# State space mixer rebuilt: parameters made in earlier stages, input scaled after its transfer through memory, three of its four quarters by GpSimd

## The reference, cut to what matters

```python
    return rmsnorm(x, final_g)
...
def s5_mixer(x, a_re, a_im, log_dt, b_re, b_im, c_re, c_im, d_skip, w_glu, w_out):
    u = x.astype(f32).reshape(bsz, seq, SSM_GROUPS, SSM_GROUP)      
    dt = jnp.exp(log_dt.astype(f32))[:, None]
    lam_re = jnp.minimum(a_re.astype(f32), -1e-4)
    mag = jnp.exp(lam_re * dt)
    lbar_re, lbar_im = mag * jnp.cos(lam_im * dt), mag * jnp.sin(lam_im * dt)
...
    y = y.reshape(bsz, seq, D_MODEL) + d_skip.astype(f32) * x.astype(f32)
    h = jax.nn.gelu(y)
    val, gate = jnp.split(h @ w_glu, 2, axis=-1)
    z = val * jax.nn.sigmoid(gate)
```

## Time and profile before

| | us |
|---|---|
| median of 3 runs (lowest, highest) | 4406.85 (4403.81, 4413.22) |
| the profiled execution | 4410.32 |
| its span on the core | 4408.5 |
| TensorE / VectorE / ScalarE / GpSimd busy | 4083.4 / 1918.9 / 1275.7 / 1491.3 |

### The profile page before, as it was taken

One profiled execution on the slowest core, in us unless ns is written; L12 is line 12 of the kernel. 1 busy time (PEld: TensorE's weight loads), 2 busy tenths in 40 slices (PEclk: granted clock), 3 DMA queues, 4 the chain that ended last, 5 costly groups with the idle time before them and its releaser, 6 DMA issues.

```text
span 4408.5 us, 51098 instructions
## 1 busy us (share of the span) xinstructions
PE 4083.4 (93%) x19931; PEld 3125.3 (71%) x19931; DVE 1918.9 (44%) x2148; ACT 1275.7 (29%) x1901; POOL 1491.3 (34%) x1022
## 2 busy tenths in 40 slices
PE   7998998899999989549999999998999999999998
PEld 5776774457777764448888888886666678888886
DVE  4254661326676761861263323314444455323321
ACT  3222330222222211321142232225444544223222
POOL 1430000011111118552344444443444444444443
PEclk8999999999999999779999999999999999999999
DMA  6111004311212131621223333331000022333333
GB/s 228 39 39 53 1 0 163 113 53 68 72 68 76 70 116 43 111 69 48 72 92 99 95 100 95 96 104 66 22 25 20 25 97 95 95 99 97 96 99 105
DMA packets 115674, 344.05 MB, mean 78 GB/s; under 512 B 17588, under 2 KB 35279, under 8 KB 113792
## 3 DMA queue, kind: packets, MB, share of 16 engines
q1 hardware_dynamic: 100368, 296.12, 21.6%
q0 software_dynamic: 7680, 31.54, 1.9%
q10 hardware_dynamic: 7472, 14.22, 0.9%
HBM read 315.37 MB, written 24.12 MB: 77 GB/s over the span
## 4 chain that ended last, share of the span: by engine, by line
PE 61%; issue 17%; DVE 9%; POOL 8%; ACT 2%; DMA 2%; POOLq 0%; ACTq 0%; SPq 0%; DVEq 0%
PE banks L274 21%; PE banks L2937 6%; POOL w_parts L259 6%; PE banks L1214 6%; PE banks L288 5%; PE banks L692 5%; PE banks L1572 4%; PE banks L978 3%; PE banks L3011 2%; DVE neg_max L1057 2%; PE banks L3040 1%; PE banks L3027 1%; PE banks L1553 1%; DMA w_ring<-in_weights 1%; PE banks L1602 1%
## 5 line engine op out<-in xcount | busy, mean ns | idle before, releaser
L259 POOL TENSOR_TENSOR w_parts<-w_ring,w_parts 128x1024 fp32r<-128x1024 f32 x344 | 835.3, 2429 | 1128.3 <-ACT w_parts L252 1128.3
L274 PE MATMUL banks<-x_high,w_parts 128*128 128x512 f32 x2944 | 911.9, 390 | 0.0
L252 ACT ACTIVATE w_parts<-w_ring 128x1024 fp32r<-128x1024 f32 x344 | 364.5, 1060 | 1292.1 <-PE banks L274 1284.7
L274 PEld LDWEIGHTS banks<-x_high,w_parts 128*128 128x128 f32 x2944 | 552.6, 188 | 116.5 <-issue 2.1
L274 PE MATMUL banks<-x_low,w_parts 128*128 128x512 f32 x1472 | 572.7, 389 | 0.0
L274 PE MATMUL banks<-hidden_high,w_parts 128*128 128x512 f32 x1600 | 482.0, 391 | 6.0 <-POOL w_parts L259 6.0
L3145 DVE TENSOR_TENSOR_SCAN arena<-arena,flags 128x128 f32<-128x128 f32 (+3 forms) x192 | 229.7, 1200 | 285.9 <-ACT arena L3086 284.4
L274 PEld LDWEIGHTS banks<-hidden_high,w_parts 128*128 128x128 f32 x1600 | 301.8, 189 | 70.9 <-POOL w_parts L259 6.8
L274 PEld LDWEIGHTS banks<-x_low,w_parts 128*128 128x128 f32 x1472 | 276.3, 188 | 59.3 <-issue 1.9
L1214 PE MATMUL banks<-parts_b,w_ring_low 128*128 128x512 f32 x896 | 303.7, 406 | 13.6 <-DVE resid_low L391 9.7
L2829 DVE TENSOR_TENSOR hidden_high<-banks,gate_temps 128x512 f32 (+1 forms) x88 | 60.9, 692 | 571.9 <-PE banks L274 571.8
(11 more groups left out here) (431 smaller groups left out, 6597.6 us busy)
## 6 DMA issues: line engine op xcount, KB each, us to landing
w_ring<-in_weights SPq DMA_DIRECT2D x488, 512.0 KB, 3.5
arena<-in_hy_dft SPq DMA_DIRECT2D x11, 1536.0 KB, 6.2
resid<-in_xT ACTq DMA_DIRECT2D x2, 2048.0 KB, 25.6
resid<-in_xT POOLq DMA_DIRECT2D x1, 4096.0 KB, 13.7
arena<-in_fn_seq POOLq DMA_DIRECT2D x1, 4096.0 KB, 17.2
resid_spill<-resid POOLq DMA_DIRECT2D x1, 4096.0 KB, 12.4
hidden<-resid_spill POOLq DMA_DIRECT2D x1, 4096.0 KB, 15.8
s_in<-hidden SPq DMA_DIRECT2D x4, 1024.0 KB, 9.8
```

Of the source, the lines that this page charges most:

```text
L252: nc.scalar.activation(WP[:, g % 2, 0, :], WR[:, (g % RING) * TILE:(g % RING + 1) * TILE], ACT.Identity).then_inc(w_hi, 1)
L259: nc.gpsimd.tensor_tensor(WP[:, g % 2, 1, :], WR[:, (g % RING) * TILE:(g % RING + 1) * TILE], WP[:, g % 2, 0, :].bitcast(F32), ALU.subtrac ...
L274: mm = nc.tensor.matmul(PS[:, bank + h // H, :], w[a][:, k % KB, :], srcs[b][:, k, at + h:at + h + H], start=(first and i + q == 0), stop= ...
```

## The change

- **Parameters early.** The computation of `S5Prep` moves from GpSimd at 1650 us to VectorE in `EvOut` (`denominator`, `angle`, `coefficients`, `powers_c(0)`, `steps`), before the norm `n_x1` (`phases(0)`) and in `Fourier` (the other quarters). GpSimd's queue keeps each result in DRAM (`keep`) and loads them back in `OdOut` and `S5`. The table `hy_dft` is loaded in `Fourier` after the last `keep`; before, at the start of `EvOut`.
- **Sums of squares.** VectorE adds the squares of `OdOut`'s tiles up; TensorE sums them once after the last tile, in token order and in the order by chunks (`RINV8`).
- **Scale late.** ScalarE writes the unscaled tiles (times `final_g`) into `R` right after each tile, and SP sends three quarters to memory during `OdOut`. They are read back into `XT`, and there multiplied by `RINV8`: quarter 0 by VectorE, quarters 1 to 3 by GpSimd (`normed`).
- **`inputs`** for all four quarters run in `OdOut`, into buffers of their own; the first `turned` stands before tile 7.
- **`ssm_d`** enters as 64 small products in `kernels`; the gelu is applied when the outputs are copied out; `skip` and the second gelu are gone.
- **Order of SP:** all reads of the inputs, then `toeplitz(0)`; for each quarter the outputs go out before `toeplitz(q+1)`.
- The residual for the layer norm goes to memory before the mixer (4 MB, GpSimd's queue) and comes home after it (SP's queue); VectorE scales it then.

```diff
@@ norm_stage, dve_parts (n_x1)
             def dve_parts(v_, link):
+                S5Prep.phases(v_, link, 0)
                 wait_done(v_, after)
...
@@ EvOut.dve, after tile n
+                if n == 0:
+                    S5Prep.denominator(v, link)
+                if n == 1:
+                    S5Prep.angle(v, link)
+                if n == 3:
+                    S5Prep.coefficients(v, link)
                 if n in (4, 6):
                     HyPrep.angles(v, link, n // 2 - 2)
+                if n == 4:
+                    S5Prep.powers_c(v, link, 0)
+                if n == 5:
+                    S5Prep.steps(v, link)
...
@@ HyPrep.pool, Fourier.pool
-            g.dma_start(ar(B_TAB, 8 * 512), ins["hy_dft"][:, 0:8 * 512]).then_inc(dft_in, 16)
+            S5Prep.params(g)
+            S5Prep.keep(g, "small")
+            S5Prep.keep(g, "cl", 0)
...
             for j in range(6):
                 Paired.weight_low(g, j)
+                if j in (2, 3, 4):
+                    S5Prep.keep(g, *(("cl", 1), ("e", 1), ("cl", 2))[j - 2])
+            S5Prep.keep(g, "e", 2)
+            S5Prep.keep(g, "cl", 3)
+            S5Prep.keep(g, "e", 3)
+            g.wait_ge(pre_kept, 48 + 64)
+            g.wait_ge(pre_kept_e, 64)
+            g.dma_start(ar(B_TAB, 8 * 512), ins["hy_dft"][:, 0:8 * 512]).then_inc(dft_in, 16)
...
@@ S5Prep
+        def keep(g, what, q=0):
+            k = ["small", ("cl", 0), ("e", 0), ("cl", 1), ("e", 1), ("cl", 2), ("e", 2), ("cl", 3), ("e", 3)]
+            g.wait_ge(pre_made, k.index((what, q) if what != "small" else what) + 1)
...
+            elif what == "cl":
+                g.dma_start(cl_dram[q], ar(22016, QP * 288)).then_inc(pre_kept, 16)
...
@@ Fourier.dve
+            S5Prep.powers_c(v, link, 1)
+            S5Prep.phases(v, link, 1)
+            S5Prep.powers_c(v, link, 2)
             for b in range(0, 8, 2):
                 v.wait_ge(f_ab, b + 1)
                 nc.vector.tensor_copy(FAB[:, b, :], PS[:, 4 + b % 4, :]).then_inc(f_abd, 1)
+            S5Prep.phases(v, link, 2)
+            S5Prep.powers_c(v, link, 3)
+            S5Prep.phases(v, link, 3)
...
@@ OdOut.pe
             for n in range(8):
                 matmul_tile(p, OdOut.st, n, n, M1)
-                if n:
-                    sums(n - 1)
-            sums(7)
+                if n == 6:
+                    S5.turned(p, 0)
+            p.wait_ge(s5_vbt, 4)
+            for i, sq in enumerate((ACC_SQ, SQ)):
...
+                for t in range(CK):
+                    mm = nc.tensor.matmul(PS[:, 4, 0:NC], PARTS_OF_ONES[:, 112 - 16 * t:240 - 16 * t], sq[:, t:T:CK],
+                                          start=(i + t == 0), stop=(i == 1 and t == CK - 1), skip_group_check=True)
...
@@ OdOut.act, after tile n
+                nc.scalar.activation(R[n // 2 % 2][:, n % 2, :].rearrange("p (s c) -> p s c", s=CK),
+                                     HT[:, n, :].rearrange("p (c s) -> p s c", s=CK), ACT.Identity,
+                                     scale=vec("final_g", n)).then_inc(s5_r, 1)
...
@@ OdOut.dve, after tile n
+                if 1 <= n <= 6:
+                    OdOut.waits(v, "sq_ready", n + 1)
+                    nc.vector.tensor_tensor(ACC_SQ, ACC_SQ, SQ[:, :], ALU.add).then_inc(n_sem["sq_free"], 1)
+                if n < 4:
+                    S5.inputs(v, link, n)
...
@@ S5.sp
+            for e in range(E0, E0 + 8 + RING):
+                load(e)
+                if e - E0 in (5, 7, 9):
+                    inputs_out((e - E0 - 5) // 2)
+            inputs_in(0)
+            inputs_out(3)
+            for q in range(1, 4):
+                inputs_in(q)
+            s.wait_ge(s5_zero, 4)
             toeplitz(0)
-            for q in range(4):
-                u_in_out(q)
+            s.wait_ge(spilled, 80)
             for q in range(4):
-                if q < 3:
-                    toeplitz(q + 1)
                 s.wait_ge(s5_ye, 4 * (q + 1))
...
+                if q < 3:
+                    toeplitz(q + 1)
+                s.wait_ge(y_out, 16 * CK * (q + 1))
...
+            s.dma_start(XT, spill).then_inc(x_home, 16)
 
@@ S5.pool
+            g.wait_ge(s5_vt, 4)
+            phases_in(1)
+            wait_done(g, OdOut.done)
+            g.dma_start(spill, HT).then_inc(spilled, 16)
+            OdOut.waits(g, "mean_in", 1)
+            magnitudes(0)
+            S5.normed(g, nc.gpsimd, 1)
+            S5.normed(g, nc.gpsimd, 2)
+            g.wait_ge(s5_vt, 8)
+            magnitudes(1)
+            S5.normed(g, nc.gpsimd, 3)
+            for q in (2, 3):
+                g.wait_ge(s5_st, q - 1)
+                phases_in(q)
+                magnitudes(q)
+                powers_in(q)
 
+        def normed(waits, engine, q):
+            waits.wait_ge(u_in, 16 * CK * (q + 1))
+            if q:
+                waits.wait_ge(s5_un, q)
+            u = XT_[:, 16 * q * NC:16 * (q + 1) * NC].rearrange("p (g c) -> p g c", g=16)
+            engine.tensor_tensor(u, u, RINV8.unsqueeze(1).broadcast_to([P, 16, NC]), ALU.mult).then_inc(s5_un, 1)
...
@@ S5.dve
+            link(nc.vector.reciprocal(RINV8, RINV8))
+            S5.normed(v, nc.vector, 0)
+            v.wait_ge(u_out, 64)
+            S5.chain(v, link, 0)
+            S5.chain(v, link, 1)
+            S5.chain(v, link, 2)
+            S5.chain(v, link, 3)
+            v.wait_ge(s5_st, 4)
+            for k in range(KB):
+                low(k)
+            link(nc.vector.reciprocal(RINV[:, :], RINV[:, :]))
+            v.wait_ge(x_home, 16)
+            for k in range(KB):
+                nc.vector.scalar_tensor_tensor(XT[:, k, :], XT[:, k, :], vec("final_g", k), RINV[:, :],
+                                               ALU.mult, ALU.mult).then_inc(n_sem["scaled"], 1)
...
@@ S5.act, in quarter 3 before its outputs
+                    a.wait_ge(s5_tp, 16 * CK * 4)
+                    for j in (-2, -1):
+                        round_ahead(a, PLAN["glu"], j)
+                    for k in range(4):
+                        high(k)
...
@@ S5.pe
+                    for par in range(2):
+                        b = 2 * par + j // 4
+                        mm = nc.tensor.matmul(PS[0:16, b, (j % 4) * P:(j % 4) * P + 16], IDENT[32:48, 32:48],
...
-                    return PS[:, 2 * par + j // 4, (j % 4) * NC:(j % 4 + 1) * NC]
+                    return PS[:, S5.bank(q) + 2 * par + j // 4, (j % 4) * NC:(j % 4 + 1) * NC]
```

More of the change, by code:

```diff
@@ L1279, in pool @@
             g.dma_start(spill, XT).then_inc(spilled, 16)
+            S5Prep.keep(g, "e", 0)
         def products(p, i):
@@ new lines, in _build @@
+    pw_dram = nc.dram_tensor("s5_pw", (P, 576), F32, kind="Internal").ap()
+    m8_dram = nc.dram_tensor("s5_m8", (P, 32), F32, kind="Internal").ap()
+    s5p_in, s5_ang, s5_sin = (sem("s5_" + x) for x in ("par", "ang", "sin"))
+    pre_made, pre_kept, pre_kept_e = (sem("s5_" + x) for x in ("made", "kept", "kept_e"))
+    s5_r, u_out, u_in, s5_zero, s5_un = (sem("s5_" + x) for x in ("r", "u_out", "u_in", "zero", "un"))
+    s5_cl, s5_e, s5_vb, s5_k, s5_km, s5_tp = (sem("s5_" + x) for x in ("cl", "e", "vb", "k", "km", "tp"))
@@ L1946, in _build @@
+    CLS = [ar(14848 + QP * 288 * i, QP * 288, **cl_shape) for i in range(2)]
+    ACC_SQ = ar(19456, T)
+    PARTS_OF_ONES = ar(20480, 240)
+    M8_, RINV8 = ar(20720, 32), ar(20752, NC)
+    RV, TV = ar(20976, 2048, **e_shape), ar(23024, 2048, **e_shape)
+    R = [ar(20976 + 2048 * i, 2048, "p (k t) -> p k t", k=2) for i in range(2)]
+    STT_ = ar(25072, 2 * QP * (NC + 1), "p (i j c) -> p i j c", i=2, j=QP)
+    TP = ar(27136, 2048, "p (g n) -> p g n", g=16)
     class OdOut(Stage):
@@ L2207, in _build @@
-    TCL = take(QP * 9 * 16)
-    S.insert(S.index(OdOut) + 1, S5Prep)
     class S5(Stage):
@@ L2350, in dve @@
-            low(7)
+            tt = nc.vector.tensor_tensor
+            def low(k):
+                v.wait_ge(s5_hi, k + 1)
+                if k == 3:
+                    v.wait_ge(s5_y, 16)
+                tt(PTA[:, 1, k, :].rearrange("p (c t) -> p c t", t=CK), HT[:, k, :].rearrange("p (t c) -> p c t", t=CK),
+                   PTA[:, 0, k, :].bitcast(F32).rearrange("p (c t) -> p c t", t=CK), ALU.subtract).then_inc(s5_part, 1)
+            OdOut.waits(v, "root", 1)
+            link(nc.vector.reciprocal(RINV8, RINV8))
@@ L2374, in act, with results @@
-            for k in range(KB):
-                OdOut.waits(a, "scaled", k + 1)
-                nc.scalar.activation(HT[:, k, :].rearrange("p (s c) -> p s c", s=CK),
-                                     XT[:, k, :].rearrange("p (c s) -> p s c", s=CK), ACT.Identity).then_inc(s5_r, 1)
+            def results(q):
+                for n, (b, g0) in enumerate(PARITY_BANKS):
+                    a.wait_ge(s5_y, 4 * q + n + 1)
+                    nc.scalar.activation(XT_[:, :].rearrange("p (g c) -> p g c", c=NC)[:, 16 * q + g0:16 * q + g0 + 7:2, :],
```

(12 more changed lines are left out.)

599 lines of the change are left out of this document (296 added, 303 removed).

## The result

| | before | after |
|---|---|---|
| median of 4 runs each (lowest, highest), us | 4408.67 (4403.81, 4413.22) | 4365.48 (4364.9, 4369.62) |
| span of the profiled execution, us | 4408.5 | 4363.0 |
| OdOut starts | 1650.5 | 1656.0 |
| T, end of the last tile | 1770.9 | 1767.9 |
| y0, y3 | 1835.3, 1953.5 | 1836.7, 1915.9 |

The ratio is 0.9904, with a 95% interval from 0.9887 to 0.9921: 1.0% faster. The forecast was 4354.0, so 11.5 us too low, and 7.3 us too low by the spans (4355.7 against 4363.0); the result lies inside the forecast's range, 4345 to 4366, by half a microsecond. By the marks: the front of the kernel loses 5.5, the tiles of `OdOut` give 8.5, T to y0 costs 4.5, the loop gives 39.1 and the tail 8.0, together -45.6; the spans differ by 45.5.

The account below looks back on a forecast made before the run. The mixer was where time must be earned: TensorE worked 91 of 170 us there. Gains 8.3 - 0.6 + 40.2 + 4.9 + 0 = 52.8 us, off the median 4406.85, gave 4354.0 us; own range 4345 to 4366.

Parts of the forecast that it names:

- Tiles: In OdOut, sums of squares leave the row of tiles and 16 transposes enter it: gain 8.3 us.
- The loop: From quarter 0's outputs to quarter 3's: GpSimd's waits go, SP's transfers bind; 78 us for 118.2, gain 40.2.
- T to y0: From OdOut's last tile to quarter 0's outputs: early input waits behind other reads; 65 us against 64.4, cost 0.6.
- issued to T + 51.5, landed at T + 54: In SP's queue after OdOut, toeplitz(0) stands behind all four input reads and lands 54 us after the last tile.
- The residual's part: After OdOut, the residual's 4 MB delay quarter 0's reading: back at T + 21, against T + 11 without contention.
- The scale on GpSimd: Beside the chains, GpSimd's scale takes 4.0 us against VectorE's 2.4 and is hidden; uncovered, 3 x 4 us.
- GpSimd and VectorE hinder each other: Rival in the chains: three GpSimd scales stretch VectorE's operations and come late, 13 us in all, 4367 us; chance 0.09.
- The tail: From quarter 3's outputs to the first Glu tile's end: 26.5 us against 31.4, gain 4.9.
- cold TensorE: In the tail, before the first Glu tile ends, a TensorE gone cold adds 2.5 us.
- The front: Early parameter steps and table load in EvOut, Fourier and before Hyena: 0 us net, from -3 to +6.
- pushes Hyena's first rows back 2 to 3 us: Just before Hyena, the 2 MB table hy_dft now loads and delays the stage's first rows by 2 to 3 us.
- 2 to 3 back: At EvOut's start, where the table no longer loads beside the weights, some 2 to 3 us are gained.

Follow-up runs that it names:

- e1: Changed kernel with quarters 1 to 3 scaled by VectorE, each after the previous quarter's chain, instead of by GpSimd: 4369.1 us, ratio to before 0.9906.
- e2: Changed kernel with toeplitz(0) issued ahead of the readings of quarters 1 to 3: 4359.0 us, ratio to before 0.9889.
- e5: Changed kernel with the table hy_dft loaded behind Hyena's first rows and W3 instead of ahead of them: 4363.7 us, ratio to before 0.9903.
- e8: Changed kernel with toeplitz(0) ahead of readings 1 to 3 and VectorE scaling inside the chains: 4351.3 us, ratio to before 0.9873.
- e9: Changed kernel with VectorE scaling inside chains, residual written in three pieces, toeplitz(0) between readings 2 and 3, hy_dft behind Hyena's first rows: 4345.6 us, ratio to before 0.9849.
- e3: Changed kernel with the residual's 4 MB sent after GpSimd's third scale instead of at T + 2: 4357.1 us, ratio to before 0.9884.

## Why the prediction was right, and where it wasn't

**Tiles.** -8.5 for -8.3: right, with tiles end to end and T 111.9 us after the start. No run undoes this part or the tail's; both rest on the rows alone.

**The loop.** 79.1 for 78, gain 39.1 for 40.2. Cause and size hold: putting GpSimd's work back costs 36.5. SP's writes and `toeplitz` run back to back and part 1 waits for them, 26.4 us apart on average for 26. In chains 2 and 3 no wait for GpSimd is left. That the number came so near is in part luck. From y to the start of part 1 a quarter took 18.5, 17.4 and 16.8 us for the 16.5 of the sum, 3.2 us more in all, and the products 26.4 for 28.5. And in the other profiles that leave the loop's work and order as they are (e1, e2, e5, e8, e9) it took 79.3 to 88.0.

**T to y0.** Forecast 65, measured 68.9. The step that failed is `toeplitz(0)` "issued to T + 51.5, landed at T + 54". Quarters 0 and 1 were back a little sooner than I put them (T + 19.9 for 21, T + 30.0 for 31), but quarters 2 and 3 later (T + 42.5 for 41, T + 54.1 for 51). SP was free for `toeplitz` at T + 46, while the last reading was still under way; its eight transfers then took 6.8 us to issue, which I had nearly left out, and landed 5.6 us after that, 4.5 after the last reading, where I had given 3. So of the 4.6 us that `toeplitz(0)` was late, 3.1 are the readings' and 1.5 its own. That the early input is spent behind the other reads is right: moving `toeplitz(0)` forward and taking GpSimd off the chain gave 10.7 us. The residual's part, 4 MB against the readings, is right in direction: 6 us by e3, for the 10 (T + 21 against T + 11) that the sum held. That quarter 0 came back near T + 21 is luck in part, since two errors nearly cancel: without the 4 MB it is back at T + 14 and not T + 11. Nor was the T + 23 of both transfers in full reached: the 4 MB took 19.6 us instead of 12.4, so both gave way.

**The scale on GpSimd.** It took 4.52 us, for 4.0. "Hidden" is right for this order (e1). The rival "GpSimd and VectorE hinder each other" named the right engines and the wrong mechanism. I stretched operations 2.9 times and got 2.6 us a scale, and 1.6 for GpSimd's lateness; in truth one operation is stopped until the scale is over, which alone costs 4.2. That my total, 3 x 4.2 = 13 us, meets the 12.6 measured on chain 0 is luck. It did become the bound, not in the changed kernel but in e2, where `toeplitz(0)` no longer was.

**The tail.** 23.5 for 26.5, gain 8.0 for 4.9. The steps up to the last reading back took 15.0 us for 15.1. After it the sum held 8.9 us for `high`, `low` and products, and 2.5 for a cold TensorE, together 11.4; measured, 8.5. TensorE had six of eight blocks done before, as it had before the change, and began the other two after one `high` and one `low` (3.9 us), with the second pair beside it; the sum counted both `high`. The cold TensorE was there: the last two blocks took 4.5 us (1934.81 to 1939.33) at a mean granted clock of 0.66, as they did before (4.54), and at the rate of the 22 products in the next 4.67 us, at full clock, their twelve would take 2.5. So that term was about right, by this estimate 2.0 for 2.5.

**The front.** Forecast 0, measured +5.5 between the two profiles, and it makes most of the miss. 2.3 of it is there before the change's first instruction: `EvOut` starts at 671.1 for 668.8. Over the eight profiles with this same front it starts at 668.0 to 671.7, so this is spread between executions. From `EvOut`'s start to `OdOut`'s took 981.7 us before and 978.5 to 985.3 in those eight, on average 983.2: 1.5 us more, with one profile of the kernel before to set against a spread of 7. The interval with the table's load, which varies far less (39.1 to 40.6 for 37.8 before), holds 2.1 more on average, and giving the rows the way takes 2 back: with the table behind, `EvOut` to `OdOut` took 981.3 on average of four. So the forecast's "pushes Hyena's first rows back 2 to 3 us" is right; what failed is the credit of "2 to 3 back" at the start of `EvOut`. Its first wait for weights fell from 8.60 us to 6.42, but a later one grew from 1.62 to 2.87, and no gain at its end can be told from the spread. The early steps themselves are covered: in `Fourier` two of the 18 operations of `powers_c` took 3.47 and 3.41 us beside `weight_low`, the others 1.36, and VectorE was free at 941.9, before the 944 asked for.

Together: +5.5 front, -0.2 tiles, +3.9 y0, +1.1 loop, -3.1 tail is 7.2 of the 7.3 us between forecast and span. The other 4.2 us of the miss on the median are the base: the forecast's median lay 1.7 us below its span, as the first runs of the kernel before had it, and the measured one lies 2.5 above.

## What to carry to other kernels

Before moving work to an engine off the path, look at what the path's engine will run beside it. GpSimd's scale was free while a transfer was late and cost 4.2 of its 4.5 us each time in the next version, once that transfer was in time. When a transfer stands in a queue behind others that aren't due, its place can cost more than its length: `toeplitz(0)`, 7 us long, came forward, the scale left GpSimd, and y0 came 10.7 us sooner. And a difference at the far end of a 4 ms kernel is best read between marks that the change can touch, since two executions of the same code were 4 us apart before it began.
